# Expert weights of a hybrid decoder layer on Trainium2: gate and up loaded in halves of the contraction rows, four gate groups before four up groups

## The chip, the cores and the metric

The kernel runs on one core of a Trainium2 chip. A core has TensorE (PE in the profile; its weight loads are PEld), VectorE (DVE), ScalarE (ACT), GpSimd (POOL) and SyncE (SP), which run their own instruction streams and meet at semaphores. 16 DMA engines move data between HBM and the on-chip memories: SBUF, with 128 partitions, and PSUM, with 8 banks in each partition, into which PE writes. The metric is the device time of one execution in microseconds, the median of several runs; lower is better.

## The reference

One layer of a decoder for 1024 prompt tokens and 64 sample tokens, 1088 in all, with 1024 features, in 32-bit floats. Cut to what matters here:

```
h = RMSNorm(x);  proj = h @ w_in                     # pooling mixer and gated linear attention
x = x + concat(a, b) @ w_out
h2 = RMSNorm(x)
group of a token = top 1 of 4;  experts = top 2 of the 4 in that group, with weights c
for each of the 16 experts:
    y = (silu(h2 @ w_gate[e]) * (h2 @ w_up[e])) @ w_down[e]     # w_gate, w_up: 1024 x 512; w_down: 512 x 1024
    acc = acc + c[:, e] * y
output = RMSNorm(x + acc)
```

The kernel computes an expert only for the tokens routed to it.

## The kernel before

Three parts follow each other: the mixers (not touched), `b2_all` (output projection, norm, router), and `b3_all` (the experts, one step each, with more steps if an expert has more than 160 tokens; here 16 steps run).

**Routing part (`b2_all`).** Tokens come in nine tiles of 128 rows (`TT`, the last has 64). For each tile VectorE writes the scaled, normed rows `h2` (L1595; for the last tile in two halves, `scaled`, L1583) in SBUF, and SP stores them to `h2_dram`, from which the experts fetch rows later. In the same loop VectorE copies the router's partial sums (L1540) and adds the residual (L1563); PE transposes that sum (L1351, for the router) between projection matmuls (L1399 to L1401). The first expert's weights are loaded in this part. After the last tile comes a chain of small VectorE operations that makes the routing tables.

**Expert step (`b3_all`, `step`).** A step handles up to W = 160 tokens: 128 whole rows in `xg`, and up to 32 left-over rows, fetched as four chunks of 256 features in `xg2`. PE transposes them into `xT`, eight blocks of 128 features by 160 tokens. Block k holds the features 128k to 128k+127. Then:

- **Gate and up.** The 512 hidden columns are four groups f of 128. `gate_up(f, side)` (L1908) makes 8 matmuls over k into one half of `bank[f % 2]`, 128 x 160 each; the profile has two records for each of them. For each f: gate, then up. ScalarE takes silu of the gate half into `sg` (L2008), VectorE multiplies by the up half into `hid` (L2148), ScalarE and VectorE split `hid` into a rounded part and a rest, `hs` (L2014, L2111).
- **Between.** PE makes the row indices of the step after next (`indices`, L1893) and transposes the next step's rows (`rows_in`, L1900, L1905), which VectorE copies into `xT` (L2102, L2105).
- **Down.** The left-over rows first (`left_down`, L1933, into bank 1), then the whole rows in three matmuls per k and half (`down`, L1922 to L1924, into banks 2 and 3). ScalarE and VectorE split w_down beforehand (L2012, L2116). VectorE adds the results to the old rows (L2183, L2188), GpSimd sends them.

**Weights.** `ring` has four units of 1 MB, `wdn` two. `expert_unit` says which piece of an expert goes into which unit: u = 0 and 1 are gate and up for the first 256 hidden columns, 2 and 3 for the last 256, each as eight pieces of 256 floats (1 KB) in a partition; 4 and 5 are w_down. SP issues units 0 and 1 of the next expert when two groups are done, 2 and 3 when four are, 4 and 5 when `left_down` and the split of w_down are.

**Order and queues.** The order on each engine is that of the code in `step`; no scheduler moves it. GpSimd's indirect DMAs (row fetches L1807, sends L1820) have a queue of their own, beside SP's. VectorE copies `lists_now` (L2164) once GpSimd's previous sends have landed (`e_free`); after it come the next lists, the one-hot matrix (L2050) and then the sums L2183 and L2188. PE waits on `e_z` for these sums before it writes the banks again.

## Time and profile before

| | |
|---|---|
| Median of 3 runs | 877.75 us (877.45 to 877.90) |
| The profiled execution | 877.90 us, its span 877.94 us |
| Busy: PE, PEld, DVE, ACT, POOL | 96%, 85%, 60%, 44%, 28% of the span |
| Expert steps | 16 from 431.92 us on, most of them 26.84 us |
| Gate and up matmuls (L1912) | 2048 records, 286.1 us busy |
| DMA | 118,505 packets, 95,928 of them under 2 KB, 17,012 of those under 512 B; 166.56 MB |

The profile is one execution. Its times are microseconds from the first instruction. A busy share is an average over parts with different limits, so the expert steps are read one at a time: which engine is busy without a gap, what the others wait for, and what the chain of work that ended last runs through. "Idle before" an instruction tells how long its engine stood still and who released it.

### The profile page before, as it was taken

How to read it: one execution, taken by the hardware profiler on the slowest of the kernel's cores; microseconds unless marked ns; L12 is line 12 of the kernel's file. 1: busy time of each engine (PE TensorE's matmuls, PEld its weight loads, DVE VectorE, ACT ScalarE, POOL GpSimd, SP SyncE). 2: the span in 40 equal slices, each digit the busy share in tenths (PEclk: the TensorE clock that was granted, in tenths of full speed). 3: DMA queues.
4: the chain of work that ended last, by engine and by line, in shares of the span. 5: the costliest groups of instructions: out<-in, count | busy, mean ns of one | idle time of the engine just before them, and what ended most of it. 6: DMA issues, size and time to landing. Idle time of an engine off the chain costs nothing.

```text
span 877.9 us, 15841 instructions
## 1 busy us (share of the span) xinstructions
PE 845.3 (96%) x5828; PEld 749.4 (85%) x5828; DVE 526.8 (60%) x1237; ACT 383.5 (44%) x734; POOL 244.6 (28%) x272
## 2 busy tenths in 40 slices
PE   6999999999999999998899999999999999999993
PEld 5989879999988787775789988889988999888992
DVE  5537424657778435557585676656666656766573
ACT  7545303656367425544334434344343444433442
POOL 1000000000000110002045654447545555445472
PEclk9999999999999999999599999999999999999997
DMA  9121001102222182336188889978899887898871
GB/s 291 43 97 47 2 0 49 49 1 56 49 96 96 59 274 91 150 145 216 60 275 290 300 304 325 306 271 310 291 310 324 307 288 278 290 360 295 286 256 50
DMA packets 118505, 166.56 MB, mean 190 GB/s; under 512 B 17012, under 2 KB 95928, under 8 KB 118469
## 3 DMA queue, kind: packets, MB, share of 16 engines
q1 hardware_dynamic: 103109, 135.48, 45.7%
q0 software_dynamic: 15360, 30.59, 10.2%
q8 instruction: 24, 0.39, 0.2%
q14 instruction: 12, 0.10, 0.0%
HBM read 146.84 MB, written 41.17 MB: 214 GB/s over the span
## 4 chain that ended last, share of the span: by engine, by line
PE 47%; another core or an unknown queue 1%; ACT 1%; issue 1%; DVE 0%; POOL 0%; ACTq 0%; POOLq 0%
PE bank L1912 31%; PE bank L1922 4%; PE bank L1933 3%; PE bank L1924 3%; PE bank L1923 3%; PE bank L1900 2%; PE bank L1893 1%; ACT split L2012 1%; POOL out L1820 0%; PE bank L1905 0%; DVE wdlo L2116 0%; PE bank L1939 0%; DVE x L2188 0%; ACT hs L2014 0%
## 5 line engine op out<-in xcount | busy, mean ns | idle before, releaser
L1912 PE MATMUL bank<-big,ring 128*128 128x160 f32 x2048 | 286.1, 301 | 0.1
L1912 PEld LDWEIGHTS bank<-big,ring 128*128 128x128 f32 x2048 | 281.9, 191 | 1.4
L1836 POOL TENSOR_TENSOR hold_at<-ident 128x1 f32<-128x1 f32 x63 | 53.1, 842 | 175.3 <-DVE lists L2083 128.4
L2116 DVE TENSOR_TENSOR wdlo<-wdn,split 128x1024 fp32r<-128x1024 f32 x64 | 76.7, 1219 | 0.0
L2008 ACT ACTIVATE sg<-bank 128x160 f32<-128x160 f32 x64 | 19.5, 304 | 109.7 <-PE bank L1912 95.4
L2012 ACT CAST split<-wdn 128x1024 fp32r<-128x1024 f32 x64 | 64.9, 1039 | 0.0
L502 PE MATMUL bank<-split,ring_r 128*128 128x384 f32 (+1 forms) x192 | 64.4, 336 | 0.1
L504 PE MATMUL bank<-split,ring_r 128*128 128x384 f32 (+1 forms) x192 | 61.7, 321 | 0.0
L2111 DVE TENSOR_TENSOR hs<-hid,hs 128x128 fp32r<-128x128 f32 x64 | 18.9, 295 | 57.3 <-ACT hs L2014 46.8
L1922 PE MATMUL bank<-split,hs 128*128 128x512 f32 x128 | 52.6, 411 | 0.0
L1399 PE MATMUL bank<-split,ring_r 128*128 128x512 f32 (+1 forms) x128 | 51.7, 404 | 0.3 <-PEq L1191 0.3
L1924 PE MATMUL bank<-split,hs 128*128 128x512 f32 x128 | 50.3, 393 | 0.0
L1923 PE MATMUL bank<-wdlo,hs 128*128 128x512 f32 x128 | 50.3, 393 | 0.0
L1400 PE MATMUL bank<-split,ring_r 128*128 128x512 f32 (+1 forms) x128 | 50.1, 392 | 0.0
L1401 PE MATMUL bank<-split,ring_r 128*128 128x512 f32 (+1 forms) x128 | 49.9, 390 | 0.0
L2017 ACT ACTIVATE squares<-z 128x256 f32<-128x256 f32 x16 | 6.7, 417 | 98.8 <-DVE z L2183 86.7
L2148 DVE TENSOR_TENSOR hid<-sg,bank 128x160 f32<-128x160 f32 x64 | 20.5, 320 | 48.1 <-ACT sg L2008 44.3
L1255 POOL MEMSET chunk<- 32x1 f32 x4 | 0.4, 92 | 169.7 <-POOLq L1191 169.5
L2050 DVE TENSOR_TENSOR big<-iota_w,rank_m 128x2304 bf16<-128x2304 f32 x17 | 43.5, 2560 | 0.0
L1820 POOL DMA_INDIRECT out<-ot,lists_now x32 | 37.6, 1174 | 10.0 <-issue 10.0
L502 PEld LDWEIGHTS bank<-split,ring_r 128*128 128x128 f32 x192 | 36.1, 188 | 0.9 <-ACT uT L713 0.3
L504 PEld LDWEIGHTS bank<-split,ring_r 128*128 128x128 f32 x192 | 36.0, 188 | 0.0
(390 smaller groups left out, 1788.4 us busy)
## 6 DMA issues: line engine op xcount, KB each, us to landing
wdn<-in_w_down SPq DMA_DIRECT2D x32, 1024.0 KB
ring<-in_w_gate SPq DMA_DIRECT2D x32, 1024.0 KB, 5.4
ring<-in_w_up SPq DMA_DIRECT2D x32, 1024.0 KB
ring<-in_w_in SPq DMA_DIRECT2D x8, 1024.0 KB, 5.9
x<-in_x_prompt SPq DMA_DIRECT2D x8, 512.0 KB, 6.1
h_rows<-h SPq DMA_DIRECT2D x8, 512.0 KB, 2.6
sums<-x SPq DMA_DIRECT2D x8, 512.0 KB, 3.6
v<-in_x_prompt SPq DMA_DIRECT2D x4, 512.0 KB, 5.4
```

Of the source, the lines that this page charges most:

```text
L502: nc.tensor.matmul(out, whi, hi[:, k, :], start=k == 0, stop=False)
L504: mm = nc.tensor.matmul(out, wlo, hi[:, k, :], start=False, stop=k == KC - 1)
L1399: nc.tensor.matmul(out, ahi[:, s, k, 0:r], whi[:, k, :], start=k == 0, stop=False)
L1400: nc.tensor.matmul(out, ahi[:, s, k, 0:r], wlo[:, k, :], start=False, stop=False)
L1401: m = nc.tensor.matmul(out, alo[:, s, k, 0:r], whi[:, k, :], start=False, stop=k == KC - 1)
L1836: nc.gpsimd.tensor_tensor(hold_at[:], ident[:, 0:1], ident[:, 1:2], ALU.add).then_inc(e_hold, 1)
L1912: x = nc.tensor.matmul(bank[f % 2][:, side * 256:side * 256 + W], ring[:, u, k, c0:c0 + P], xT[:, k, :], start=k == 0, stop=k == KC - 1)
L1922: nc.tensor.matmul(bank[2 + h][:, :], hi, whi, start=k == 0, stop=False)
L1923: nc.tensor.matmul(bank[2 + h][:, :], hi, wlo, start=False, stop=False)
L1924: x = nc.tensor.matmul(bank[2 + h][:, :], lo, whi, start=False, stop=k == 3)
L2012: nc.scalar.copy(wdhi[:, k, :], wdn[:, k // 2, (k % 2) * D:(k % 2 + 1) * D]).then_inc(e_wh, 1)
L2116: nc.vector.tensor_tensor(wdlo[:, k, :], wdn[:, k // 2, (k % 2) * D:(k % 2 + 1) * D], wdhi[:, k, :].bitcast(F32), ALU.subtract).then_inc(e ...
```

## The change

The contraction rows are dealt out in another way. Partition p now holds the features 8p to 8p+7, where it held p, 128 + p, 256 + p and so on. A partition's share of a gate or up matrix is then 8 rows that lie side by side in HBM, 16 KB; a unit of `ring` takes half of it, four rows, as one run of 8 KB. Units 0 and 1 are the two halves of gate, 2 and 3 those of up. To match, `h2` is written in turned order, feature 8q + k at place 128k + q, so that block k of `xT` has the features that partition by partition meet the weights.

A half holds all 512 hidden columns for four of the eight k. So the groups run in another order: four gate groups, then four up groups, each with 8 matmuls into a bank of its own (`bank[f]`), the up group into the bank that its gate group had, after the silu. `sg` has four buffers. The product waits for PE's up group, the splits of w_down and of `hid` stand in another order, and in the first step the two later list preparations come ahead of VectorE's products.

```
 def expert_unit(A, ring, wdn, u, e):
     if u < 4:
-        w = (A["w_gate"], A["w_up"])[u % 2].rearrange("l e (k p) n -> (l e) p k n", p=P)
-        return ring[:, u, :, :], w[e, :, :, (u // 2) * 256:(u // 2 + 1) * 256]
+        w = (A["w_gate"], A["w_up"])[u // 2].rearrange("l e (p h k) n -> (l e) p h k n", p=P, h=2)
+        return ring[:, u, :, :].rearrange("p (k a) n -> p k (a n)", k=4), w[e, :, u % 2, :, :]

 routing part, VectorE
+def by_lane(t):  return t.rearrange("t (q k) -> t q k", k=KC)
+def turned(t):   return t.rearrange("t (k q) -> t q k", k=KC)
-                nc.vector.scalar_tensor_tensor(out=h2[0:r, j % 2, :], in0=x1[0:r, j, :], scalar=rstd[0:r, j:j + 1],
-                                               in1=g2b[0:r, :], op0=ALU.mult, op1=ALU.mult).then_inc(r_h2, 1)
+                nc.vector.scalar_tensor_tensor(out=turned(h2[0:r, j % 2, :]), in0=by_lane(x1[0:r, j, :]),
+                                               scalar=rstd[0:r, j:j + 1], in1=by_lane(g2b[0:r, :]), op0=ALU.mult,
+                                               op1=ALU.mult).then_inc(r_h2, 1)
 (scaled(h), the two 512-feature halves of the last tile, likewise)

 SP
-                    sp.wait_ge(e_gu, i * 4 + (2 if u < 2 else 4))
+                    sp.wait_ge(e_gu, i * 8 + (4 if u < 2 else 8))

 PE
+        def gate_or_up(i, side, f):
             for k in range(KC):
+                if f == 0 and k % 4 == 0:
+                    pe.wait_ge(e_w[2 * side + k // 4], i * 16 + 16)
+                x = nc.tensor.matmul(bank[f][:, 0:W], mats[:, side, k, f * P:(f + 1) * P], xT[:, k, :],
                                      start=k == 0, stop=k == KC - 1)
+            x.then_inc(e_gu, 1)
         def step(i, first, last):
             pe.wait_ge(e_xe, i * 3 + 3)
             for f in range(4):
+                if f >= 1 and not first:
+                    pe.wait_ge(e_z, i * 3 + f // 3)
+                gate_or_up(i, 0, f)
                 ...
+            for f in range(4):
+                pe.wait_ge(e_si, i * 4 + f + 1)
+                gate_or_up(i, 1, f)

 ScalarE
+                nc.scalar.activation(sg[:, f, :], bank[f][:, 0:W], ACT.Silu).then_inc(e_si, 1)     # four in a row
+            weights_hi(0)
+            weights_hi(1)
+            gated_hi(0)
+            weights_hi(2)
+            gated_hi(1)
+            weights_hi(3)
+            gated_hi(2)
+            gated_hi(3)

 VectorE
             if first:
                 first_lists()
+                next_lists()
+                third_table()
+            def gated(f):
+                dve.wait_ge(e_gu, i * 8 + f + 5)
+                nc.vector.tensor_tensor(hid[:, f, :], sg[:, f, :], bank[f][:, 0:W], ALU.mult).then_inc(e_h, 1)
+            weights_lo(i, 0)
+            gated(0)
+            weights_lo(i, 1)
+            gated_lo(i, 0)
+            ...
+            gated(3)
+            gated_lo(i, 3)
```

PE in a middle step, before: from the first gate and up group on. "big" is the memory in which `xT` lies, `ssq3` and `same` make the left-over rows' sum of squares; a row with x15 stands for 15 instructions like the one above it.

```order
L1912 MATMUL bank0<-big,ring 128x160 [waits e_w1,e_w0]
L1912 MATMUL bank0<-big,ring 128x160 x15
L1939 MATMUL bank6<-ssq3,same 128x1 [waits e_sql]
L1950 REGISTER_ALU [waits e_h]
L1912 MATMUL bank1<-big,ring 128x160 [waits e_z]
L1912 MATMUL bank1<-big,ring 128x160 x15
L1945 REGISTER_ALU
L1912 MATMUL bank0<-big,ring 128x160 [waits e_w3,e_w2,e_h]
L1912 MATMUL bank0<-big,ring 128x160 x15
```

The same place with the change (line numbers of the changed kernel; L1923 is its gate or up matmul, L1948 the sum of squares), from the second half of the first gate group to the first up group.

```order
L1923 MATMUL bank0<-big,ring 128x160 [waits e_w1]
L1923 MATMUL bank0<-big,ring 128x160 x3
L1923 MATMUL bank1<-big,ring 128x160 [waits e_z]
L1923 MATMUL bank1<-big,ring 128x160 x7
L1948 MATMUL bank6<-ssq3,same 128x1 [waits e_sql]
L1923 MATMUL bank2<-big,ring 128x160 [waits e_z]
L1923 MATMUL bank2<-big,ring 128x160 x7
L1955 REGISTER_ALU
L1923 MATMUL bank3<-big,ring 128x160 [waits e_z]
L1923 MATMUL bank3<-big,ring 128x160 x7
L1965 ISA
L1923 MATMUL bank0<-big,ring 128x160 [waits e_w2,e_si]
```

A group of 16 that made both sides has become two groups of 8, far apart; the wait for `e_z` now stands after 8 matmuls where it stood after 16, and again ahead of the third and fourth group; waits for the silus (`e_si`) are new, those for VectorE's products (`e_h`) inside gate and up are gone.

VectorE in a middle step, before: its products (L2148), differences (L2111) and w_down differences (L2116).

```order
L2148 TENSOR_TENSOR hid<-sg,bank 128x160 [waits e_si]
L2111 TENSOR_TENSOR hs<-hid,hs 128x128 [waits e_hh]
L2116 TENSOR_TENSOR wdlo<-wdn,split 128x1024 [waits e_wh]
L2147 REGISTER_ALU
L2148 TENSOR_TENSOR hid<-sg,bank 128x160 [waits e_si]
L2111 TENSOR_TENSOR hs<-hid,hs 128x128 [waits e_hh]
L2116 TENSOR_TENSOR wdlo<-wdn,split 128x1024 [waits e_wh]
```

With the change (L2172 the product, L2130 the difference, L2135 that of w_down):

```order
L2135 TENSOR_TENSOR wdlo<-wdn,split 128x1024 [waits e_wh]
L2171 ISA
L2172 TENSOR_TENSOR hid<-sg,bank 128x160 [waits e_gu]
L2134 REGISTER_ALU
L2135 TENSOR_TENSOR wdlo<-wdn,split 128x1024 [waits e_wh]
L2130 TENSOR_TENSOR hs<-hid,hs 128x128 [waits e_hh]
L2171 REGISTER_ALU
L2172 TENSOR_TENSOR hid<-sg,bank 128x160 [waits e_gu]
```

The product waits for PE (`e_gu`) instead of ScalarE's silu (`e_si`), and each w_down difference stands ahead of the small difference instead of behind it.

## Rows read from the trace of the kernel before

**Rows 1.** Windows view, one step: length, busy per engine (records), clock, DMA share, GB/s
```profile
541.31:568.15 26.84, 26.84 (x215) 24.62 (x214) 16.54 (x42) 11.14 (x23) 13.26 (x14) 1.00 0.87 292
```

**Rows 2.** Chain of waits, in that step: start, length in us, what
```profile
545.93 13.15 PE bank L1912 x96
...
559.51 0.93 PE bank L1900 x8
```

**Rows 3.** Windows view, PE's gate and up matmuls (L1912) alone
```profile
541.31:545.66 4.35, 4.35 (x32) 1.00 1.04 413
546.01:558.92 12.91, 12.91 (x96) 1.00 0.65 200
...
568.15:595.92 27.77, 17.77 (x129) 1.00 0.83 295
676.44:703.28 26.84, 17.77 (x129) 1.00 0.92 325
703.28:731.16 27.88, 17.77 (x129) 1.00 0.89 304
```

**Rows 4.** Waits of PE from 440 to 856 us: total, times, longest
```profile
PE bank L1933 <- DVE hid L2148: 1.9, 2, 1.0
```

**Rows 5.** Windows view, w_down loads alone, then gate and up loads alone
```profile
541.31:543.31 2.00, 2.00 (x16) 2.00 (x15) 1.21 (x4) 1.23 (x4) 1.70 (x2) 1.00 1.04 414
563.31:565.31 2.00, 2.00 (x10) 1.63 (x9) 1.42 (x12) 0.00 (x0) 0.00 (x0) 1.00 1.08 347
```

**Rows 6.** Timeline, ScalarE in a step: start, length, operation [idle before]
```profile
547.66 0.30 ACT L2008 ACTIVATE sg<-bank 128x160 f32<-128x160 f32 x1
547.86 1.04 ACT L2012 CAST split<-wdn 128x1024 fp32r<-128x1024 f32 x1
```

**Rows 7.** Timeline, VectorE: a usual step's first sum, then the tight step
```profile
541.40 0.74 DVE L2188 SCALAR_TENSOR_TENSOR x<-bank,weight_now,x 128x512 f32<-128x512 f32 x1
...
671.56 0.17 DVE L2164 COPY lists_now<-lists_next 128x8 int32<-128x8 int32 x1 [0.79 <-POOLq L1872]
...
677.51 0.74 DVE L2188 SCALAR_TENSOR_TENSOR x<-bank,weight_now,x 128x512 f32<-128x512 f32 x1
```

**Rows 8.** Timeline, the last step after gate and up
```profile
856.33 0.30 ACT L2008 ACTIVATE sg<-bank 128x160 f32<-128x160 f32 x1 [1.97 <-issue]
856.87 0.32 DVE L2148 TENSOR_TENSOR hid<-sg,bank 128x160 f32<-128x160 f32 x1
...
857.24 1.93 PE L1933 MATMUL bank<-wdn,hid 128*32 128x256 f32 x32 [0.95 <-issue]
```

**Rows 9.** Timeline, the silu that came late in the step from 703.28
```profile
718.38 0.30 ACT L2008 ACTIVATE sg<-bank 128x160 f32<-128x160 f32 x1 [4.55 <-remote]
```

**Rows 10.** Timeline of the routing part: a regular tile, the tight tile, the last
```profile
376.66 0.69 DVE L1563 TENSOR_TENSOR x<-x,bank 128x512 f32<-128x512 f32 x1 [1.11 <-PE bank L1401]
...
395.15 3.60 POOL L1284 TENSOR_TENSOR uT<-keys,bmask 64x2048 f32<-64x2048 f32 x1 [85.20 <-DVE ring_r L1547]
395.33 4.51 DVE L1595 SCALAR_TENSOR_TENSOR h<-x,rstd,g2b 128x1024 f32<-128x1024 f32 x1
...
400.68 0.42 PEld L1351 LDWEIGHTS bank<-ident,x 128*128 128x128 f32 x4 [0.33 <-DVE x L1563]
...
402.44 1.28 DVE L1595 SCALAR_TENSOR_TENSOR h<-x,rstd,g2b 128x1024 f32<-128x1024 f32 x1
...
406.38 0.68 DVE L1563 TENSOR_TENSOR x<-x,bank 64x512 f32<-64x512 f32 x1 [1.22 <-PE bank L1401]
...
408.59 0.22 DVE L1540 COPY big<-bank 128x64 f32<-128x64 f32 x1 [0.54 <-PE bank L1365]
```

**Rows 11.** Timeline, VectorE operations with hopping destination, with hopping sources
```profile
420.93 0.29 DVE L1683 TENSOR_SCALAR rank_m<-big 128x135 f32<-128x135 f32 x1
...
423.03 0.41 DVE L1696 TENSOR_TENSOR big<-big 128x144 f32<-128x144 f32 x1
```

**Rows 12.** Windows view, first expert step, where PE's clock is half
```profile
429.00:435.20 6.20, 6.13 (x40) 5.99 (x41) 3.35 (x16) 2.73 (x4) 0.00 (x0) 0.50 0.35 107
```

More of the change, by code:

```diff
@@ L124, in expert_rows, with by_lane, turned @@
     return t.rearrange("t (c d) -> (t c) d", d=CW)
+def by_lane(t):
+    return t.rearrange("t (q k) -> t q k", k=KC)
+def turned(t):
+    return t.rearrange("t (k q) -> t q k", k=KC)
 def program(nc, A, O):
@@ L1581, in scaled @@
         def scaled(h):
-            link(nc.vector.tensor_tensor(h2[0:NS, 0, h * 512:(h + 1) * 512], x1[0:NS, TT - 1, h * 512:(h + 1) * 512],
-                                         g2b[0:NS, h * 512:(h + 1) * 512], ALU.mult))
+            lanes = slice(64 * h, 64 * h + 64)
+            link(nc.vector.tensor_tensor(turned(h2[0:NS, 0, :])[:, lanes, :], by_lane(x1[0:NS, TT - 1, :])[:, lanes, :],
+                                         by_lane(g2b[0:NS, :])[:, lanes, :], ALU.mult))
         for i in range(TT):
@@ L1944, in step @@
             for f in range(4):
-                pe.wait_ge(e_h, i * 4 + (1 if f < 2 else f))
-                if f % 2 == 0:
-                    pe.wait_ge(e_w[f], i * 16 + 16)
-                    pe.wait_ge(e_w[f + 1], i * 16 + 16)
-                if f == 1:
-                    pe.wait_ge(e_z, i * 3 + 1)
-                gate_up(f, 0)
-                gate_up(f, 1)
-                if first and f == 0:
+                if f >= 1 and not first:
+                    pe.wait_ge(e_z, i * 3 + f // 3)
+                gate_or_up(i, 0, f)
+                if first and f == 1:
                     pe.wait_ge(e_oh, 2)
@@ L1956, in step @@
                     indices(facts)
-                if f == 0 and not first:
+                if f == 1 and not first:
                     pe.wait_ge(e_sql, i)
                     left_sums()
+            for f in range(4):
+                pe.wait_ge(e_si, i * 4 + f + 1)
+                gate_or_up(i, 1, f)
             if not last:
@@ L2006, in step, with weights_hi, gated_hi @@
             for f in range(4):
-                act.wait_ge(e_gu, i * 4 + f + 1)
-                nc.scalar.activation(sg[:, f % 2, :], bank[f % 2][:, 0:W], ACT.Silu).then_inc(e_si, 1)
-                for k in ((0,), (1,), (2, 3), ())[f]:
-                    if k % 2 == 0:
-                        act.wait_ge(e_w[4 + k // 2], i * 16 + 16)
-                    nc.scalar.copy(wdhi[:, k, :], wdn[:, k // 2, (k % 2) * D:(k % 2 + 1) * D]).then_inc(e_wh, 1)
+                act.wait_ge(e_gu, i * 8 + f + 1)
+                nc.scalar.activation(sg[:, f, :], bank[f][:, 0:W], ACT.Silu).then_inc(e_si, 1)
+            def weights_hi(k):
+                if k % 2 == 0:
+                    act.wait_ge(e_w[4 + k // 2], i * 16 + 16)
+                nc.scalar.copy(wdhi[:, k, :], wdn[:, k // 2, (k % 2) * D:(k % 2 + 1) * D]).then_inc(e_wh, 1)
+            def gated_hi(f):
                 act.wait_ge(e_h, i * 4 + f + 2)
                 nc.scalar.copy(hs[:, f, 0, :], hid[:, f, 0:P]).then_inc(e_hh, 1)
+            weights_hi(0)
[6 more added lines that the diff above has]
+            gated_hi(3)
             nc.scalar.activation(warm[:], eps_c[:], ACT.Sqrt)
@@ L2145, in step @@
                 first_lists()
-            for f in range(4):
-                dve.wait_ge(e_si, i * 4 + f + 1)
-                nc.vector.tensor_tensor(hid[:, f, :], sg[:, f % 2, :], bank[f % 2][:, 256:256 + W],
-                                        ALU.mult).then_inc(e_h, 1)
-                if first and f == 0:
-                    next_lists()
-                if first and f == 1:
-                    third_table()
-                if last and f == 1:
-                    nc.vector.tensor_tensor(S0[:], S0[:], samples.added, ALU.add).then_inc(e_state, 1)
-                gated_lo(i, f)
-                for k in ((0,), (1,), (2, 3), ())[f]:
-                    weights_lo(i, k)
+                next_lists()
+                third_table()
+            if last:
+                nc.vector.tensor_tensor(S0[:], S0[:], samples.added, ALU.add).then_inc(e_state, 1)
+            def gated(f):
[5 more added lines that the diff above has]
+            gated_lo(i, 0)
+            gated(1)
+            weights_lo(i, 2)
+            gated_lo(i, 1)
+            gated(2)
+            weights_lo(i, 3)
+            gated_lo(i, 2)
+            gated(3)
+            gated_lo(i, 3)
             if not last:
```

10 lines of the change are left out of this document (2 added, 8 removed).

## The prediction

> **What bounds the kernel now.** I read the stretches cut at the step boundaries first, then the chain of waits, and last the waits of single engines. PE's busy share of the whole span says little by itself; one expert step says more. From 541.31 to 568.15 us PE is busy for all of the 26.84 us, VectorE for 16.54, ScalarE for 11.14 [rows 1]. The chain through that step is PE alone: after the first 32 gate-and-up matmul records come 96 in 13.15 us, then from 559.08 the index products, from 559.51 the transposes [rows 2], and the down products until the next step begins. So steps 1 to 14 are a PE stream with no room in it; only two are longer, 27.77 us from 568.15 and 27.88 from 703.28 [rows 3]. In all of these steps PE waited for another engine twice, 1.9 us together, both times for VectorE's product of gate and up, and never for a transfer [rows 4].
>
> That is the main reading. The 16 DMA engines are 87% busy in a step [rows 1], but nothing on PE ends on them. A change that makes loads cheaper moves a resource that is busy and not late.
>
> **The loads.** Gate and up are 4 MB a step. They move in 1 KB runs. While only such runs are served, 347 GB/s pass; while only the 4 KB rows of w_down are served, 414 [rows 5]. No data run of 8 KB stands in this trace, so 414, the nearest, is my value for it. 4.19 MB at 347 is 12.1 us, at 414 it is 10.1: some 2 us of DMA time less in each step, or nothing if the runs are cut up. All of it is off the path: PE never waits for a load [rows 4], and ScalarE's first copy of w_down follows its silu at 547.86 with no idle time before it [rows 6]. Value: 0 us, whichever holds. The first pair of loads (now both gate halves) is issued where the first pair was (one gate and one up piece), the second pair likewise, and each pair is needed at the same point of the step, so no deadline gets shorter.
>
> **PE's own stream.** The same 128 matmul records a step, of the same size. What is new is where they stop to look at a semaphore: three places inside gate and up before, nine after. 96 records with two such stops in them take 12.91 us, or 134 ns a record; the 32 ahead of them with none take 4.35, or 136 ns [rows 3]. A satisfied wait costs nothing that shows. Upper bound: the chain has 13.15 where 96 times 136 ns is 13.05 [rows 2], 0.1 us for two stops and the return from the small sum product; six more stops would be 0.3 us a step at that price, 4.5 us over 15 steps. I take 0, since the equal pace is the nearer row.
>
> **Are the new waits satisfied?** Bank 1 and bank 2 are now needed by the second and third gate groups, so PE waits at 2.17 us into a step (16 records of 136 ns) until VectorE has read the first half of the previous result, and at 6.5 us for the other half. Before, it waited for both at 4.35. The tightest step I found begins at 676.44 [rows 3]; VectorE's first sum there ends at 677.51 + 0.74 = 678.25, PE asks at 678.61, so 0.36 us is left. In a usual one, from 541.31, it ends at 542.14 and PE asks at 543.48: 1.34 us are left [rows 7]. The up groups wait for the silus: the first silu, behind its table load, runs at 547.66, 6.35 us into the step [rows 6], and the first up group starts at 8.7. Four silus of 0.30 us are done by 9.1, the fourth is needed at 15.2. Value: 0.
>
> **VectorE and ScalarE inside a step.** Each up group lasts 2.17 us, and in it VectorE has one product (0.32), one weight difference (1.22) and one small difference (0.29), 1.83 us; ScalarE has 1.04 + 0.30. So VectorE keeps pace, and its last product ends some 0.4 us after the last up group instead of after a silu as well. In a middle step PE is still in the index products and transposes then, so this hides entirely. In the last step there are none: the silu runs at 856.33, VectorE is in weight differences until the product at 856.87, and PE starts the left-over rows at 857.24 after 0.95 us idle [rows 8]. With the silu long done and no difference queued ahead, the product follows the matmuls directly: 856.87 - 856.33 = 0.54 us sooner. What is late next is PE itself. **-0.5 us.**
>
> **The two long steps.** The excess is 0.93 + 1.04 = 1.97 us [rows 3]. In the step from 703.28 a silu was released late, at 718.38, by something the profile calls remote, with 4.55 us of idle time before it [rows 9], though PE's records run on at their pace; the one from 568.15 looks alike. PE then idled up to 1.0 us [rows 4]. If the semaphore of a group arrives late again, it matters less: a late gate group has 2 us and more to spare, a late third up group is absorbed (VectorE has 0.3 us to spare per group and 1.4 us until PE's transposes end), a late fourth one still costs. Half of these places are now harmless, so I take half of the excess: **-1.0 us**, between 0 and -2.
>
> **Rows written in turned order.** Eight VectorE writes of 1024 elements and two of 512 now step 512 bytes between elements. They take 1.28 us each, like the one at 402.44 [rows 10]. The nearest rows differ: the one at 420.93, whose destination hops 9 words every element, takes 0.29 us for 135 elements; the one at 423.03, whose two sources hop 16 words, takes 0.41 for 144 [rows 11]. The difference, less 0.01 for nine elements, is 0.11 us, 0.7 ns an element. So 0 to 0.7 us for 1024. I take 0.7, since 16 words is the nearer step to 128. Most of it hides: VectorE sits idle 1.11 us before its residual sum in a regular tile, at 376.66. One tile has no room. At 395.33 the write takes 4.51 us, because GpSimd's 3.60 us operation began at 395.15, and PE starts its transposes at 400.68, released by the residual sum that follows [rows 10]. So 0.7 us there goes to the end. In the last tile the write and the first 512-element write add 1.05 us ahead of the sum at 406.38, which sits 1.22 us idle for PE; the second one adds 0.35 ahead of the copy at 408.59, with 0.54 idle [rows 10]. Both fit. **+0.7 us**, from 0 up.
>
> The Trainium skill (Vector Engine (DVE) Microarchitecture Reference, section 5.2 on measured stream behaviour) says that a destination that hops every element runs at 1.71 to 2.5 ns a column where contiguous ones take 1.05. That would be 0.7 to 1.5 us on 1024 elements, an estimate from that page; this case's nine-word row disagrees with it, and no row here has the 512-byte step. By its upper figure the time would be that of rival 2.
>
> **Sum.** The profiled execution spans 877.94 us, 0.2 above the median of the three timed runs, 877.75; both count from the first to the last instruction, so I apply the terms to the median: 877.75 - 0.5 - 1.0 + 0.7 = 877.0 us.
>
> **Rivals.**
> 1. *GpSimd's transfers are served later (slower).* VectorE may not overwrite its row lists before GpSimd's results have landed: ahead of the tight step it waited 0.79 us for that, at 671.56 [rows 7]. These results are sent while the gate loads run. If an 8 KB run holds a DMA engine twice as long as a 4 KB row and GpSimd's packets take turns with it, they land later. In the tight step 0.36 us of delay is enough to stop PE, in a usual one 1.34. If a delay of 2 us finds 4 tight steps and 11 usual ones, the cost is 4 x 1.64 + 11 x 0.66 = 14 us, 891. Against it: the loads finish 2 us sooner, w_down ends sooner, so GpSimd's sums and old rows start sooner. Chance 0.10. The Trainium skill (DMA: Bandwidth & Descriptors, section on queues, rings and completion order) has each engine go round its queues packet by packet, a rule that speaks for this rival; no run here yet shows 8 KB packets.
> 2. *Strides cost double (1.4 us on 1024).* Then the tight tile gives 1.4, the last tile adds 2.1 over a cover of 1.22, and the late 512-element write 0.7 over 0.54: 1.4 + 0.9 + 0.2 = 2.5 instead of 0.7, 878.8. For it: a long power-of-two step. Against: the nine-word row. Chance 0.10.
> 3. *PE's half clock lasts longer (slower).* PE is granted 0.50, its 1.2 GHz level, from 429.0 to 435.2, in the first expert step after the routing in which it idled [rows 12]. A restart moved by 0.7 us could meet the return of the clock at another moment; another 6 us at half speed costs 3 us, 880.0. Chance 0.06.
> 4. *The stops cost their upper bound (slower).* 877.0 + 4.5 = 881.5. Chance 0.04.
> 5. *No late semaphore, free strides (faster).* 877.75 - 0.5 - 2.0 = 875.2. Chance 0.15.
> 6. *The loads stay as slow as before.* If the runs are cut up, DMA share stays at 87% and the time is the forecast's, since nothing waits for them. Inside the forecast.
>
> **How the numbers follow.** The forecast has 0.55, its own range 875.9 to 878.9 (late semaphores 0 to -2, strides 0 to 0.7 and a little). 0.2% is 1.76 us, about what a measurement of this kernel can tell from no change: faster means below 876.0, slower above 879.5. Faster: rival 5 and the forecast's low edge, 0.16. Slower: rivals 1, 3, 4 and the tail of 2, 0.22. Same: 0.62. The range 875.0 to 880.3 leaves out rivals 1 and 4 and the low tail of rival 5, under 2 in 10.
>
> **What would show it.** In the profile after: steps of 26.84 us still, PE fully busy in them; few packets under 2 KB and a DMA share some 7 points lower, with no gain from it; the write of the turned rows at 2.0 us; PE at the left-over rows of the last step 0.4 us after its last up group. Wrong would be: an idle time of PE before the second gate group, steps well under 26.84, or a routing part that ends more than 2 us later.

## The result, and the profile after

The changed kernel takes **893.4 us** (median of 4 runs, 890.55 to 898.92) against 877.83 for the kernel before: a ratio of 1.0175, 95% interval 1.0149 to 1.0202. It is slower by some 15 us, far above the 880.3 that ended the range. The profiled run is the fastest of the four; it took 890.55 us and spans 888.8. In later series one execution of the kernel before and one each of e5 and e6 took over 4000 us; the ratios leave them out. Below, a time within a step counts from the step's first gate matmul.

First the page of the changed kernel: busy shares, packets, the first queue's share.

```profile
PE 850.8 (96%) x5828; PEld 753.5 (85%) x5828; DVE 531.4 (60%) x1237; ACT 386.9 (44%) x734; POOL 257.2 (29%) x272
...
DMA packets 61161, 166.56 MB, mean 187 GB/s; under 512 B 17012, under 2 KB 30392, under 8 KB 52933
...
q1 hardware_dynamic: 45765, 135.48, 42.1%
```

The loads do what the diff says: 8 KB packets. The shares of the engines tell as little as they did before. The cut by steps does (windows view, PE's gate and up matmuls alone: window, length, busy, clock, DMA share, GB/s; answers to [rows 3]).

```profile
460.40:487.24 26.84, 17.77 (x129) 17.52 (x128) 1.00 0.82 307
487.24:521.00 33.76, 20.57 (x129) 19.94 (x128) 0.90 0.67 244
...
547.84:574.68 26.84, 17.77 (x129) 17.52 (x128) 1.00 0.82 303
...
601.52:631.11 29.59, 18.04 (x128) 17.55 (x128) 1.00 0.75 275
631.11:662.04 30.93, 19.64 (x128) 19.15 (x128) 0.94 0.73 258
```

Eleven of the fourteen middle steps last 26.84 us. Three are longer, by 6.92, 2.75 and 4.09: 13.76 us together. The balance of the two profiles closes on it: +13.76, the two long steps of before gone (-1.97), the last step shorter (38.88 instead of 39.42, -0.54), and what lies ahead of the second step shorter by 0.39: +10.86, and the spans differ by 888.8 - 877.94 = 10.86. The slower three of the four runs have no trace, so this accounts for the profiled run, 10.86 us, and not for the 15.6 between the medians.

What ends the idle time in the long steps (waits from 440 to 870 us, PE and VectorE: total, times, longest; answers to [rows 4, 7]):

```profile
PE bank L1923 <- DVE x L2215: 8.8, 3, 4.1
PE bank L1942 <- DVE hid L2172: 0.4, 1, 0.4
...
DVE lists_now L2191 <- POOLq L1883: 17.8, 7, 5.9
```

PE waits at the second gate group for VectorE's sum of the step before, which the prediction had called satisfied. VectorE in turn waits for GpSimd to free the row lists. One step, from send to stop, in the chain of waits (start, length, what):

```profile
472.22 2.04 POOL out L1831
474.26 0.30 issue
474.57 1.63 POOL out L1831
476.20 0.30 issue
476.50 1.84 POOL out L1831
478.34 0.31 issue
478.65 8.06 DMA out<-ot,lists_now
...
486.88 0.17 DVE lists_now L2191
...
489.79 2.57 DVE big L2069
...
492.94 0.67 DVE x L2215
493.61 0.04 issue
493.65 4.63 PE bank L1923 x16
```

Two things stand out. Three of the four sends of results, which take 0.98 to 1.02 us elsewhere, take 1.63 to 2.04 here. And the last one needs 8.06 us from its start to the release of the lists. The rest follows: VectorE copies the lists 26.48 us into the step instead of 20.3, writes its one-hot tile, and its first sum comes after PE has asked. From the copy at 486.88 to the end of that sum at 493.61 it is 6.73 us, and PE asks 2.17 us into the next step. So, in a step of 26.84 us, lists copied later than 26.84 + 2.17 - 6.73 = 22.3 us stop PE. With the wait at 4.35 us, where the kernel before has it, the same estimate gives 24.5. (Later runs bear the first figure out: the one list copy of e5 behind it, at 23.29, and the one of e11, at 23.46, are each followed by that profile's one long step.) PE stands 4.08, 2.48 and 2.22 us, and pays again afterwards: the granted clock fell to its lower level, and 16 matmul records take 4.63 and 4.05 us instead of 2.17 behind the first and the third of these stops. (Windows view, all engines, 493.65 to 500.00: the clock is the third number from the end.)

```profile
493.65:500.00 6.35, 6.35 (x28) 6.35 (x29) 2.92 (x6) 3.04 (x7) 3.65 (x5) 0.58 0.47 153
```

### The profile page after: what moved, and what is told of

Same layout as the page of the kernel before. It is cut to its first block, busy times and chain, and to the rows that moved or that the text cites. A ratio compares the mean times of both kernels' runs of the same rounds, so it can differ in the third digit from the quotient of the medians.

```text
span 888.8 us, 15932 instructions
## 1 busy us (share of the span) xinstructions
PE 850.8 (96%) x5828; PEld 753.5 (85%) x5828; DVE 531.4 (60%) x1237; ACT 386.9 (44%) x734; POOL 257.2 (29%) x272
## 4 chain that ended last, share of the span: by engine, by line
PE 29%; POOL 8%; issue 6%; DMA 4%; DVE 3%; POOLq 0%; DVEq 0%
PE bank L1923 20%; DMA out<-ot,lists_now 4%; POOL out L1831 3%; POOL hold_at L1847 2%; PE bank L1931 2%; PE bank L1942 2%; PE bank L1933 2%; PE bank L1932 2%; POOL big L1818 1%; PE bank L1911 1%; POOL sums L1831 1%; DMA old<-sums,lists_next 1%; DVE big L2069 1%; PE bank L1904 0%; POOL old L1818 0%
## 5 line engine op out<-in xcount | busy, mean ns | idle before, releaser
L1923 PE MATMUL bank<-big,ring 128*128 128x160 f32 x2048 | 290.6, 303 | 8.8 <-DVE x L2215 8.8
L1923 PEld LDWEIGHTS bank<-big,ring 128*128 128x128 f32 x2048 | 285.5, 193 | 10.9 <-DVE x L2215 9.5
L2135 DVE TENSOR_TENSOR wdlo<-wdn,split 128x1024 fp32r<-128x1024 f32 x64 | 78.0, 1219 | 68.7 <-ACT split L2020 68.7
L1831 POOL DMA_INDIRECT out<-ot,lists_now x32 | 45.4, 1417 | 10.0 <-issue 10.0
L2024 ACT CAST hs<-hid 128x128 fp32r<-128x128 f32 x64 | 19.1, 298 | 65.2 <-DVE hid L2172 65.2
L1831 POOL DMA_INDIRECT out<-x,lists_now x32 | 41.1, 1284 | 7.9 <-issue 7.9
```

What stands on the lines that cost most here:

```text
L1831: nc.gpsimd.indirect_dma_start(out=expert_rows(dst) if which else dst, in_=part, in_offset=None, bounds_check=(4 * rows if which else rows ...
L1923: x = nc.tensor.matmul(bank[f][:, 0:W], mats[:, side, k, f * P:(f + 1) * P], xT[:, k, :], start=k == 0, stop=k == KC - 1)
L2135: nc.vector.tensor_tensor(wdlo[:, k, :], wdn[:, k // 2, (k % 2) * D:(k % 2 + 1) * D], wdhi[:, k, :].bitcast(F32), ALU.subtract).then_inc(e ...
```

## Experiments: is it the long packets, the deadline, or the start?

The mechanism looked like the first rival of the prediction, so four kernels took its parts away one by one.

**8 KB runs cut into 1 KB and into 4 KB.** Each load becomes two transfers, and the waits of PE count to 32:

```diff
+    return [(dst[:, :, 256 * a:256 * a + 256], src[:, :, 256 * a:256 * a + 256]) for a in range(2)]   # 1 KB
+    return [(dst[:, 2 * b:2 * b + 2, :], src[:, 2 * b:2 * b + 2, :]) for b in range(2)]               # 4 KB
```

> The changed kernel, but each gate and up load is split into two transfers by column halves, so that its data moves in 1 KB runs again (as in the kernel before); order of the groups, waits and turned rows stay as changed. Theory A (the 8 KB packets, 309 ns each, take turns with GpSimd's 4 KB packets, 159 ns, and hold back GpSimd's old rows and results, so the row lists come late): packets of about 50 ns let GpSimd's through, VectorE's copy of the lists returns to about 20 to 21 us into every step, all steps last 26.84 us, and the time is 876 to 878 us. Rival B (the new wait at the second gate group, 2.17 us into a step instead of 4.35, is by itself too tight, whatever the loads look like): still two or three steps of 29 to 34 us, 888 to 898 us. Rival C (the different start of the expert loop after the turned rows sets off the late steps): as B.

> As e1, but each load is split into two transfers of two rows each, 4 KB runs. Theory A: GpSimd's 4 KB packets now alternate with equally long ones (159 ns) and get half of an engine instead of a third, so the lists come between the two cases, fewer or shorter late steps, 877 to 888 us. Rival B: 888 to 898 us. If only the count of transfers mattered (eight a step instead of four), e1 and e2 would give the same time.

Measured: 904.5 us (901.67 to 907.35) with 1 KB, 903.18 (901.71 to 904.96) with 4 KB. Both are slower than the 893.4 of the 8 KB runs. Theory A, as it was put, falls: it is not the length of the packets that holds back the results. (That the loads do so at any packet length is not excluded, and comes back below.) The two times are alike, as they would be if the count of transfers mattered, but the next kernel has one transfer a load and is no faster. Whether the 8 KB runs helped is not shown: 1, 2 and 4 KB runs give much the same time, and the changed kernel itself was timed in another series.

**The order of groups with plain rows.** The split of the contraction becomes (half, k, partition) and the writes of the hidden rows are those of the kernel before:

```diff
-        ... .rearrange("l e (p h k) n -> (l e) p h k n", p=P, h=2)
+        ... .rearrange("l e (h k p) n -> (l e) p h k n", p=P, h=2)
```

> The changed order of groups and waits with plain rows: the contraction rows are split (half, k, partition), so loads move in 2 KB runs and the eleven... rows of the hidden state are written unturned, exactly as in the kernel before. Theory A: 2 KB packets are short enough, all steps 26.84 us, 876 to 878 us. Rival B: 888 to 898 us. Rival C predicts a different start of the loop from e1, and the time of the kernel before or below.

Measured: 905.4 us (898.04 to 913.2). Neither the turned rows nor the run length carries the loss. It is in the new order of the groups, with its banks, its waits and VectorE's new sequence, which these kernels share.

**PE's deadline taken away.** Gate and up use banks 0, 4, 5, 1, so nothing in the first 20 us of a step overwrites what VectorE's main sums read:

```diff
+GB = (0, 4, 5, 1)
-                if f >= 1 and not first:
-                    pe.wait_ge(e_z, i * 3 + f // 3)
-                if f == 1 and not first:
+                if f == 2 and not first:
                     pe.wait_ge(e_sql, i)
```

> The changed kernel with its 8 KB runs, but the gate and up groups use PSUM banks 0, 4, 5, 1 instead of 0 to 3, so that PE needs VectorE's sums of the step before only ahead of the down products (some 20 us into a step) and the left-over rows' sum at 6.5 us; the small sum product moves from the second to the third group. Theory A in two parts: the lists stay late in some steps (25 to 27 us into the step), since the loads are the same, but PE doesn't stop for it, so every step lasts 26.84 to 27.5 us and the time is 875 to 878 us. If the lateness reaches PE another way (gathered rows late for the transposes, the left-over rows' sum late at 6.5 us), 880 to 890 us and PE idles at another line. Rival D (the half clock after the routing, not the wait, sets off the long steps): two or three long steps remain, 888 to 898 us.

Measured: 936.64 us (910.78 to 955.93), the slowest of all. The profiled run is the fastest of its four, 910.78. Its first seven middle steps last 26.86 to 26.95 us. In the eighth the lists come at 25.25 us, in the ninth not before its end, and the five after the ninth last 30 to 34 us. PE now idles at the small sum product and at the up groups (waits from 440 to 870 us):

```profile
PE bank L1951 <- ACT squares L2039: 13.2, 5, 4.5
PE bank L1926 <- ACT sg L2018: 4.5, 4, 1.9
...
DVE lists_now L2194 <- POOLq L1886: 59.4, 10, 11.0
```

So the lateness is not made by PE's stop. I read it so that the stop at the gate group let VectorE and GpSimd catch up, and that without it they fall further behind; this one kernel, which also moves the small sum product and adds two waits ahead of the transposes and the down products, does not prove it. What the early deadline does is to make a given lateness felt sooner, 22.3 instead of 24.5 us by the estimate above. Theories A and B were both wrong as they stood, and the question became what makes GpSimd's results late.

## Experiments: what GpSimd's sends meet

The timeline of VectorE and GpSimd in the same step shows it. Changed kernel, start, length, operation:

```profile
473.86 0.32 DVE L2172 TENSOR_TENSOR hid<-sg,bank 128x160 f32<-128x160 f32 x1 [0.29 <-PE bank L1923]
474.10 1.22 DVE L2135 TENSOR_TENSOR wdlo<-wdn,split 128x1024 fp32r<-128x1024 f32 x1
...
474.57 1.63 POOL L1831 DMA_INDIRECT out<-ot,lists_now  x1 [0.30 <-issue]
...
476.27 1.22 DVE L2135 TENSOR_TENSOR wdlo<-wdn,split 128x1024 fp32r<-128x1024 f32 x1
...
476.50 1.84 POOL L1831 DMA_INDIRECT out<-x,lists_now  x1 [0.30 <-issue]
...
478.65 0.98 POOL L1831 DMA_INDIRECT out<-ot,lists_now  x1 [0.31 <-issue]
```

The send begun at 474.57 ends at 476.20, 0.88 us after the difference of w_down that ended at 475.32; the one at 476.50 ends at 478.34, 0.85 after the difference that ended at 477.49. A send that meets such a difference does most of its work behind it. The kernel before has the same effect, but mostly on its last send (same view, step from 568.15):

```profile
581.54 1.02 POOL L1820 DMA_INDIRECT out<-x,lists_now  x1 [0.17 <-issue]
582.87 1.01 POOL L1820 DMA_INDIRECT out<-ot,lists_now  x1 [0.31 <-issue]
584.19 0.99 POOL L1820 DMA_INDIRECT out<-x,lists_now  x1 [0.30 <-issue]
584.24 2.35 DVE L2116 TENSOR_TENSOR wdlo<-wdn,split 128x1024 fp32r<-128x1024 f32 x2
585.48 1.97 POOL L1820 DMA_INDIRECT out<-ot,lists_now  x1 [0.30 <-issue]
```

There the send ends at 587.45, 0.86 us after the pair of differences. In the kernel before, the first two differences of a step are over by 12.0 us and the other two run back to back from 16.1; most sends lie in the gap. The change has spread them over 10.4 to 17.1 us, one beside each up group. In two of the fourteen middle steps the four sends start at 11.82, 14.17, 16.11 and 18.25 us, in a third at the same intervals from 14.57 us. How much a step suffers goes with the start: sends that begin at 9.4 to 10.3 us end at 15.8, those that begin at 11.8 end at 19.2, 3.4 us later instead of some 2. Why they begin late in some steps was not tested; in the step from 460.40 GpSimd had stood 3.43 us for its own sums to land, before it could fetch the old ones and then send.

The Trainium skill (SBUF — State Buffer, section on the two separate sides) describes this: VectorE and GpSimd share a pair of ports, one of them has it for a whole instruction, and GpSimd cannot write the descriptors of its transfers meanwhile. The traces agree that the send waits for the difference, with 0.85 to 0.88 us of work left behind it. The page's example is a one-source copy; two SBUF sources it names only against a GpSimd operation that reads SBUF, and here it is such a difference that holds up the sends.

Four kernels test that from different sides.

```diff
# e5: from the second step on, 128 of the 1024 columns
-            nc.vector.tensor_tensor(wdlo[:, k, :], wdn[...], wdhi[:, k, :]...
+            nc.vector.tensor_tensor(wdlo[:, k, 0:m], wdn[...], wdhi[:, k, 0:m]...
# e6 (and e7, on the kernel before): GpSimd's queue
+            pool.wait_ge(e_ot, i + 1) ... hold(); send_results(e_out)
             pool.wait_ge(e_sum, i * 32 + 32) ... hold(); rows_old()
-            pool.wait_ge(e_ot, i + 1) ... hold(); send_results(e_out)
# e8: the order on VectorE
+            weights_lo(i, 0); weights_lo(i, 1); weights_lo(i, 2); gated(0); weights_lo(i, 3); gated_lo(i, 0)
```

> The changed kernel, but from the second expert step on VectorE's four differences of w_down (line 2135 there) cover 128 of their 1024 columns; the other 896 keep the first expert's values, so this part of the computation is left out and the time is read with that in mind. Loads, packets, waits and the order stay. Theory E: GpSimd cannot write the descriptors of a row transfer while VectorE runs such a difference of two SBUF operands (1.22 us), and the change has spread the four of them over 10 to 17.5 us of a step, just where the four result transfers are issued; a send of 1.0 us takes 1.6 to 2.0 us there, so the transfers start at 11.8, 14.2, 16.1 and 18.3 us instead of 1.3 us apart. Without the long differences the four sends take 1.0 us each, 1.3 us apart, the copy of the lists is never later than 22.5 us, all steps last 26.84 us, and the time is 874.5 to 877 us. Theory A (the load packets hold back GpSimd's transfers): the sends may be short, but the results still land late, two or three steps stay long, 885 to 898 us.

Measured: 879.37 us (ratio 1.0012, 1.0002 to 1.0022). All sends take 0.98 to 1.12 us; PE's wait for the sums falls from 8.8 us to one of 0.9. One part of VectorE's work, on no path of its own, carries 14 of the 15.6 us. That it isn't simply a lighter VectorE, e11 below shows, which gives it more work. In one step, from 543.45, the lists are still late (23.29 us), though the last send ended at 14.93, 2.9 us ahead of the up loads:

```profile
557.39 0.99 POOL L1831 DMA_INDIRECT out<-ot,lists_now  x1 [0.30 <-issue]
561.25 0.86 SPq L1806 DMA_DIRECT2D ring<-in_w_up  x2
566.74 0.17 DVE L2191 COPY lists_now<-lists_next 128x8 int32<-128x8 int32 x1 [2.94 <-POOLq L1883]
```

So a part of the lateness has another source, which stays open.

> The changed kernel with the whole computation; on GpSimd's queue the four sends of the results go ahead of the fetch of the old sums of the next expert, instead of behind it. They are issued from about 5.7 us into a step, when their rows are ready, to about 11 us, mostly ahead of the differences (which begin at 10.4) and ahead of the first gate loads (8.7). Theory E (and A, for another reason): the results land by 15 us, the copy of the lists is at 20.3 us in every step, no step is longer than 26.84 us, 874.5 to 876.5 us, faster than both kernels. The fetch of old sums moves to 11 to 14 us and lands by 19; if it lands later than 20.3 us, VectorE's lists wait for it instead and the time is 880 to 900 us. Rival F (what sets off the late steps lies in the first routing or in PE's clock): two or three long steps remain, 885 to 898 us.

Measured: 879.12 us (ratio 1.0001, 0.9987 to 1.0014), profile 875.9. All fourteen middle steps last 26.84 us, and the sends run clear of the differences:

```profile
548.38 1.00 POOL L1831 DMA_INDIRECT out<-x,lists_now  x1 [0.54 <-issue]
549.68 0.99 POOL L1831 DMA_INDIRECT out<-ot,lists_now  x1 [0.30 <-issue]
550.98 0.98 POOL L1831 DMA_INDIRECT out<-x,lists_now  x1 [0.31 <-issue]
552.26 0.98 POOL L1831 DMA_INDIRECT out<-ot,lists_now  x1 [0.30 <-issue]
553.26 0.31 POOL L1847 TENSOR_TENSOR hold_at<-ident 128x1 f32<-128x1 f32 x1
553.72 2.02 POOL L1818 DMA_INDIRECT x<-sums,lists_next  x1 [0.15 <-issue]
```

The fetch behind them now meets the differences (2.02 us), and nobody waits for it: the lists come at 20.27 or 20.28 us in all middle steps but the first (20.50). The sends are clear of the up loads too, so this kernel does not tell the two apart; e5 and e11 do.

> The kernel before with the same exchange on GpSimd's queue. Theory E: in the kernel before the sends lie in a gap of VectorE's differences (12.0 to 16.1 us of a step) and its lists are in time, so there is little to gain: 876 to 878 us, at most the 1.9 us of the two long steps. If results_first gained for a reason that has nothing to do with the change's own order, this kernel would gain as much as that one does.

Measured: 878.4 us (ratio 0.9997, 0.9988 to 1.0007). The same edit is worth nothing in the kernel before and some 14 us in the changed one, so it repairs something that the change brought.

> The changed kernel with the whole computation; ScalarE makes its first two copies of w_down right after the third silu and the other two after the fourth, and VectorE's four differences run one behind the other from about 8.3 us to 13.2 us of a step instead of one beside each up group. GpSimd's sends then find VectorE without long differences from 13.2 us on. Theory E: the sends end by about 18.3 us wherever they start, so the copy of the lists is at 21 to 23 us in every step; PE's first sum is then still in time in most steps, 875 to 882 us, and no step shows the pattern 11.8, 14.2, 16.1, 18.3. Theory A: as the changed kernel, 888 to 898 us, or worse, since the sends would start later than its 9.4 us.

Measured: 886.1 us (881.28 to 888.51), 4 us above the range. The direction holds, the size doesn't: the sends take 0.98 to 1.02 us but start at 13.3 to 15.2 us and end at 18.2 to 20.1, and the lists come at 22.5 to 24.6, later than the 22.3 of the estimate in every step, and all steps but the first of the fourteen are longer than 26.84. Short sends that start late are not enough.

## Experiments: when a send ends

The sends of e8 point at the other half, the 8.06 us. SyncE's queue (start, length, operation) in the changed kernel and, behind it, in the kernel before, same step:

```profile
478.20 0.81 SPq L1806 DMA_DIRECT2D ring<-in_w_up  x2
```

```profile
479.27 0.37 SPq L1795 DMA_DIRECT2D ring<-in_w_gate  x1
479.74 0.53 SPq L1795 DMA_DIRECT2D ring<-in_w_up  x1
```

The last send ends at 479.63 in the changed kernel, after these loads have been issued, and its packets are seen until 486.25. In the kernel before it ends at 478.95, before them, and they are through by 479.75. The step shown has an unusually late load in the kernel before, though: the second pair comes 17.80 us into an undisturbed step of the changed kernel, and 17.94 us in ten of the fourteen middle steps before (18.45 to 19.62 in the other four).

> The changed kernel, but SyncE issues the pair of up loads (17.4 us into a step) only when PE's transposes have ended (about 20 us). Sends and differences stay as they are. Two links are told apart: the sends of 1.6 to 2.0 us (link 1), and that a send which ends after the next pair of loads has been issued lands 5 to 7 us later instead of 1 to 3 (link 2; 19.24 to 25.85 us in the step from 460.40). If link 2 holds, the late pattern 11.8, 14.2, 16.1, 18.3 still occurs, its results land at 20 to 21.5 us, the copy of the lists comes before 22.3 us and every step lasts 26.84 us: 875.5 to 878 us. If the sends' length alone is the cause, nothing changes: 888 to 898 us. If w_down now lands too late (it follows the up loads), GpSimd's sums go out later and the sends with them: 880 to 890 us.

Edit: `if u == 2: sp.wait_ge(e_xt, i * 3 + 6)` ahead of the up loads, which puts them at 19.38 us. In its profile (span 876.4 us) the slow sends are more frequent than in any other: the median of the first kind is 1.84 us, and in ten of fourteen middle steps the last one ends at 19.24. All steps are 26.84 us nevertheless. The step from 461.75:

```profile
477.86 1.84 POOL L1833 DMA_INDIRECT out<-x,lists_now  x1 [0.30 <-issue]
480.01 0.98 POOL L1833 DMA_INDIRECT out<-ot,lists_now  x1 [0.30 <-issue]
...
481.14 0.96 SPq L1808 DMA_DIRECT2D ring<-in_w_up  x2
...
483.05 0.17 DVE L2193 COPY lists_now<-lists_next 128x8 int32<-128x8 int32 x1 [0.71 <-POOLq L1885]
```

The lists come at 20.3 to 21.4 us in every step. The cleanest comparison is between steps with the same four sends, at 11.82, 14.17, 16.11 and 18.25: with the up loads at 17.80 (changed kernel, two steps) the lists come at 26.48 and 24.91, with the up loads at 19.38 (e10, six steps) at 20.5 to 20.6. So loads issued while the last send is under way cost its packets 4 to 6 us.

The converse does not hold: to end ahead of the loads is no guarantee. In the changed kernel's step from 631.11 the last send ends at 19.87 and the up loads follow at 21.89, yet the lists come at 25.23; in e5 (the three rows above) packets of a send that ended at 14.93 were seen until 22.77, and in e11, below, of one that ended at 16.22 until 22.91. Nor is an end behind the loads always dear: in the kernel before, in the step from 676.44, the last send ends at 18.20, the first load of the pair was issued at 17.94, and the lists come at 20.83. What else decides how long the results' packets take, no run here shows.

The times are split as well: three of seven runs at 878.1 to 879.9, four at 886.0 to 887.6. The median, 886.04, misses the range of link 2 and lies in that of the third branch, late w_down loads. The profile is of the first kind, so it can't tell whether that is what makes the others 8 us longer.

| Middle steps of the profile | last send ends, us | lists copied, us | long steps |
|---|---|---|---|
| before | 15.5 to 19.3 | 20.8 to 22.4 | 2, for other reasons |
| changed | 15.8 to 22.0 | 20.3 to 27.4 | 3 |
| e5, short differences | 14.4 to 17.5 | 20.3 to 23.3 | 1 |
| e6, results first | up to 12.5 | 20.3 to 20.5 | 0 |
| e10, up loads later | 15.8 to 19.2 | 20.3 to 21.4 | 0 |

**The fault put into the kernel before.** One tuple in two places moves differences 2 and 3 into the gap:

```diff
-                for k in ((0,), (1,), (2, 3), ())[f]:
+                for k in ((0,), (1, 2, 3), (), ())[f]:
```

> The kernel before, its own loads, waits and banks, with one move: ScalarE's copies and VectorE's differences 2 and 3 of w_down follow difference 1 in the second group instead of the third, so VectorE runs three long differences back to back in the stretch from about 13 to 17 us of a step, where GpSimd sends its results. Theory E: a send that meets them stands until they end, the last send ends at 19 to 20 us instead of 15.5 to 18.2, after the second pair of loads has been issued (17.9), the copy of the lists moves to 23 us or later and PE begins to wait for VectorE's sums: 883 to 900 us, though nothing of the change is in this kernel. Theories A, B and C all leave it at the time of the kernel before, 877 to 880 us.

Measured: 879.01 us median, ratio 1.0000 (0.9982 to 1.0017), but 876.8 to 887.56. The median is a miss. The profiled run is the one of 887.56, beyond all 32 runs of the kernel before beside it (up to 882.06), and shows the fault: in the steps from 569.12 and 680.58 the last send ends at 19.82 us, the lists come at 25.40 and 26.32, and the steps behind them last 30.94 and 31.86 us. Outside these steps and the ones behind them it ends by 18.32, the lists come by 22.60, and nothing is lost, although the second pair of loads is issued at 17.94 in these steps too. So what this kernel shows is that long sends are harmless in most steps and dear when the last one ends 1.5 us later; the line isn't simply whether it ends before the loads. PE asks at 4.35 us here, so lists at 22.60 are in time, which in the changed kernel would be a little late.

**Differences in four pieces of 256 columns.**

```diff
+            for q in range(4):
+                x = nc.vector.tensor_tensor(wdlo[:, k, 256 * q:256 * q + 256], ...
```

> The changed kernel with each of VectorE's 1024-column differences cut into four of 256 columns, back to back, some 0.1 us longer in all. If GpSimd gets in between two instructions of VectorE, its sends take 1.0 to 1.3 us and the time falls to 876 to 880 us; if it stands as long as VectorE has such work without a pause, the sends stay at 1.6 to 2.1 us and the time at 888 to 900 us. I expect the second: the fourth send in the kernel before took 2.0 us beside two differences run back to back.

Measured: 878.71 us (877.13 to 883.75; ratio 1.0006, 0.9991 to 1.002). My expectation was wrong, and usefully so: GpSimd gets in between two of VectorE's instructions.

```profile
580.98 1.42 DVE L2136 TENSOR_TENSOR wdlo<-wdn,split 128x256 fp32r<-128x256 f32 x4
581.03 1.25 POOL L1831 DMA_INDIRECT out<-x,lists_now  x1 [0.16 <-issue]
```

No send takes over 1.5 us, and four pieces cost VectorE 1.42 us instead of 1.22. In its profile one step is still long (28.15 us), behind lists at 23.46.

**The order of the change at its best.**

> The order of the change with plain rows and 2 KB runs (the kernel of e3), and GpSimd's results ahead of its fetch of old sums (as e6). Nothing of the turned rows and the 8 KB runs is left, so against e6 it gives their worth. Theory E: all steps 26.84 us as in e6, the last step 38.8, the routing part shorter by the 0.8 us that a turned write costs in the tight tile: 875 to 878 us, at or just below the kernel before. If 8 KB runs were worth something by themselves, this kernel would be slower than e6. If the order of the groups alone made steps late, as theory B has it, some would still be long.

It joins the edits of e3 and e6. Measured: 877.09 us (12 runs, 876.32 to 878.41), ratio 0.9984 (0.9973 to 0.9994), profile 875.0: faster than the kernel before by some 1.4 us, if by little more than the interval. Against e6 with its turned rows and 8 KB runs the ratios, 0.9984 and 1.0001 (0.9987 to 1.0014), differ by 1.5 us, but their intervals overlap and the two were measured beside different runs of the kernel before. So no worth of the 8 KB runs shows once the sends are out of the way; that the turned writes cost the 1.5 us fits and isn't shown.

## The prediction, point by point

- **Loads, 0 us.** Right for PE: DMA share 0.82 instead of 0.87 in a step, no wait for a load. The second pair is issued where it was, within 0.14 us in most steps. But the loads were taken as something that nobody but PE could feel; GpSimd's last packets do, by 4 to 6 us (changed kernel against e10).
- **PE's stops, 0 us.** Right: undisturbed steps are 26.84 us as before.
- **Are the new waits satisfied, value 0.** This is the step that failed: in the profiled run 8.8 us of waiting and about 5 more, mostly clock behind it, 4.34 of it in the 2 x 16 records behind two of the stops. The margins of 0.36 and 1.34 us were read correctly, but as if VectorE's schedule would stay where it was.
- **VectorE and ScalarE inside a step.** The true error. The spread of the differences was priced by what PE, VectorE and ScalarE wait for. GpSimd was not asked, although the trace of before held a send of 1.97 us beside a pair of differences (the row at 585.48 above) and others of 1.0. The same kind of mutual exclusion stood in [rows 10], which the prediction read in the other direction: a VectorE write of 1.28 us took 4.51 because a GpSimd operation of 3.60 had begun 0.18 us earlier.
- **Last step, -0.5 us.** Measured -0.54, and PE waits 0.4 us for VectorE's product there, as foretold.
- **Two long steps, -1.0 us.** They are absent in the profiles of the changed kernel, e6 and e12, which would be -1.97. They are absent in that of e7 too, so the order of groups need not be the reason. The term was taken off the median of runs, but the late semaphores are those of one execution; no run shows that the median contains them.
- **Turned rows, +0.7 us.** 2.08 us instead of 1.28, +0.80 for 1024 elements (row below, in the last full tile), near the estimate and under the 1.4 us of rival 2; in the tight tile 5.30 instead of 4.51. Whether the 0.8 us reached the end isn't shown: the second expert step begins at 460.40 in the changed kernel and at 460.79 in the kernel before, and with the same routing part e7 and e9 begin it at 461.86 and 461.76.

```profile
402.18 2.08 DVE L1604 SCALAR_TENSOR_TENSOR h<-x,rstd,g2b 128x1024 f32<-128x1024 f32 x1
```

- **Rival 1**, 891 us at a chance of 0.10, has nearly the right time and the right last link, the late release of the lists. Its premise, that 8 KB packets do it, is wrong: e1 and e2 took them away and the time stayed high. Its other half, that loads hold back GpSimd's results, is partly right, since e10 shows it of the second pair; alone it isn't enough, as e5, e6 and e11 leave the loads where they are and end within 0.12% of the kernel before. That its 891 us lies close to 893.4 is luck. Its price was built from the margin and an assumed delay of 2 us in all steps; in truth five of fourteen steps were 4 to 7 us late and three of them were felt.
- **Rival 3**, the half clock, was real but as a follower: it comes behind each idle time of 4.08 and 2.22 us, and not of its own accord.

With the sends out of the way the sum isn't contradicted, and not confirmed either: it asked for 0.75 us less than the kernel before, a ratio of 0.9991, and e6 has 1.0001 with an interval of 0.9987 to 1.0014. Its profile spans 875.9 us where the terms, on the profile of before, give 877.94 - 0.5 - 1.0 + 0.7 = 877.1, but that run is one of its fastest.

## To carry to other kernels

When a change moves VectorE's long operations on two SBUF sources, lay them against GpSimd's queue, and not only against the engines that read their results: look in the trace for one GpSimd transfer that takes twice its usual time and see what VectorE did beside it. Send results on GpSimd's queue ahead of what nobody waits for, and look at what is loaded while the last of them is under way. And before tuning a deadline away, ask whether the wait is the cause or what lets the others catch up.

## What the runs showed that I had not expected

- A send of 1.0 us becomes up to 2.05 us beside a 1.22 us difference; with the difference cut in four, at most 1.5.
- Two megabytes of loads, issued 0.4 us before a send begins, held its last packets back: it ended at 19.23 us and they were through at 25.85 with 8 KB packets in the loads, at 23.49 with 1 KB (e1, a step in which the sends also end at 19.23), and at 20.0 with the loads moved behind the send (e10). Why, and why some sends are slow without it, no run here shows.
- With PE's stop removed (e4) lateness grew, to steps of 34 us, where I had expected it to be absorbed.
- PE's granted clock falls to the lower level after 4.08 and 2.22 us of idling, but not after 2.48 (16 records in 2.44 us).
